# Attention's v loads: from four loads of 32 partitions to one load of 128 partitions per row group and column block

## The reference

```python
    qg = q.reshape(B, rows, GRID_W, H, dh)
    kg = k.reshape(B, rows, GRID_W, H, dh)
    vg = v.reshape(B, rows, GRID_W, H, dh)
...
        s = jnp.einsum('bqhd,brqchd->bhqrc', q_r, k_win).astype(jnp.float32) * scale + bias[None]
        p = jax.nn.softmax(s.reshape(B, H, GRID_W, wr * WIN_COLS), axis=-1)
        p = p.reshape(B, H, GRID_W, wr, WIN_COLS).astype(v.dtype)
        return jnp.einsum('bhqrc,brqchd->bqhd', p, v_win)
```

## Time and profile before

| | us |
|---|---|
| median of 3 runs (3213.3 to 3214.53) | 3214.18 |
| the profiled execution's own time | 3212.91 |
| its span in the trace | 3211.1 |
| TensorE busy in the span | 3116.0 (97%) |
| VectorE busy | 2296.2 (72%) |
| ScalarE busy | 1908.3 (59%) |

### The profile page before, as it was taken

One profiled execution on the slowest core, in us unless ns is written; L12 is line 12 of the kernel. 1 busy time (PEld: TensorE's weight loads), 2 busy tenths in 40 slices (PEclk: granted clock), 3 DMA queues, 4 the chain that ended last, 5 costly groups with the idle time before them and its releaser, 6 DMA issues.

```text
span 3211.1 us, 48845 instructions
## 1 busy us (share of the span) xinstructions
PE 3116.0 (97%) x18750; PEld 2790.3 (87%) x18750; DVE 2296.2 (72%) x3531; ACT 1908.3 (59%) x3107; POOL 187.7 (6%) x191
## 2 busy tenths in 40 slices
PE   5999999995999999999999999999999999999998
PEld 4777765785999999999999999999999999999997
DVE  4679927547777777777777777777777776777775
ACT  5154457543666666666665666666666666666654
POOL 0000000001010101010101010110101010101000
PEclk8999999997999999999999999999999999999999
DMA  9321166335666757575857576666657575857562
GB/s 333 133 66 56 50 199 237 137 119 204 240 249 239 255 211 265 200 274 193 295 201 284 211 261 230 249 248 243 247 219 257 200 277 197 295 192 287 213 248 97
DMA packets 140266, 691.17 MB, mean 215 GB/s; under 512 B 11264, under 2 KB 46352, under 8 KB 116752
## 3 DMA queue, kind: packets, MB, share of 16 engines
q1 hardware_dynamic: 130368, 661.98, 55.4%
q0 software_dynamic: 8128, 25.17, 3.2%
q10 hardware_dynamic: 1552, 1.00, 0.1%
HBM read 650.35 MB, written 37.77 MB: 214 GB/s over the span
## 4 chain that ended last, share of the span: by engine, by line
PE 75%; DVE 1%; DMA 0%; issue 0%; POOL 0%; POOLq 0%; DVEq 0%
PE psG L1671 34%; PE psG L1673 16%; PE psY L1690 5%; PE psY L1693 5%; PE psY L1691 5%; PE psY L1692 5%; PE psY L1694 5%; DMA xg<-xhat_d,isel 0%; DVE idxu L1165 0%; DVE affT L1168 0%; DVE vals L1162 0%; DVE xst L1990 0%; PE psG L1647 0%; POOL out L1736 0%; DVE yp L1938 0%
## 5 line engine op out<-in xcount | busy, mean ns | idle before, releaser
L1671 PE MATMUL psG<-xe,w_gu_hi_part 128*128 128x384 f32 x5632 | 1619.9, 358 | 2.7 <-DVE xe L2000 2.7
L1673 PE MATMUL psG<-xe,w_gu_lo_part 128*128 128x192 f32 x5632 | 1411.6, 251 | 0.0
L1673 PEld LDWEIGHTS psG<-xe,w_gu_lo_part 128*128 128x128 f32 x5632 | 1076.4, 191 | 13.1
L1671 PEld LDWEIGHTS psG<-xe,w_gu_hi_part 128*128 128x128 f32 x5632 | 1058.9, 188 | 16.5 <-DVE xe L2000 3.1
L1913 DVE TENSOR_TENSOR w_gu_lo_part<-raw_gu,w_gu_hi_part 128x1024 fp32r<-128x1024 f32 x704 | 859.3, 1223 | 119.2 <-ACT w_gu_hi_part L1795 119.2
L1795 ACT ACTIVATE w_gu_hi_part<-raw_gu 128x1024 fp32r<-128x1024 f32 x704 | 738.5, 1052 | 12.9 <-DMA raw_gu<-in_w_gu 12.9
L1823 ACT ACTIVATE low<-psG 128x384 f32<-128x384 f32 x352 | 173.0, 491 | 695.2 <-PE psG L1673 694.9
L1948 DVE TENSOR_TENSOR gu<-psG,low 128x384 f32<-128x384 f32 x352 | 196.0, 557 | 495.9 <-ACT low L1823 490.9
L1918 DVE TENSOR_TENSOR w_dn_lo_part<-raw_dn,w_dn_hi_part 128x1024 fp32r<-128x1024 f32 x352 | 431.2, 1225 | 1.0 <-ACT w_dn_hi_part L1806 0.8
L1806 ACT ACTIVATE w_dn_hi_part<-raw_dn 128x1024 fp32r<-128x1024 f32 x352 | 368.1, 1046 | 3.6 <-PE psY L1694 3.6
L1690 PE MATMUL psY<-w_dn_hi_part,hs 128*128 128x512 f32 x704 | 282.6, 401 | 0.0
(11 more groups left out here) (215 smaller groups left out, 3005.3 us busy)
## 6 DMA issues: line engine op xcount, KB each, us to landing
raw_gu<-in_w_gu SPq DMA_DIRECT2D x176, 2048.0 KB, 8.3
raw_dn<-in_w_down SPq DMA_DIRECT2D x176, 1024.0 KB, 8.6
shared<-in_ada_w SPq DMA_DIRECT2D x12, 2048.0 KB, 11.0
w_raw<-in_w_in SPq DMA_DIRECT2D x20, 512.0 KB, 5.3
bias<-in_bias SPq DMA_DIRECT2D x6, 1536.0 KB, 12.9
qk_d<-shared SPq DMA_DIRECT2D x8, 768.0 KB, 3.5
qk<-qk_d SPq DMA_DIRECT2D x8, 768.0 KB, 6.3
out<-x SPq DMA_DIRECT2D x12, 512.0 KB, 2.6
```

Source lines behind the costliest of these rows:

```text
L1671: pe.matmul(bank[:, 0:2 * CAP], wh, xe[:, k, :, :].rearrange("p a b -> p (a b)"), start=(k == 0), stop=False, skip_group_check=True)
L1673: mm = pe.matmul(bank[:, 0:CAP], wl, xe[:, k, 0, :], start=False, stop=(k == KD - 1), skip_group_check=True)
```

## The change

`load_v` now issues one DMA for one row group `n` and one column block `j`, over all 128 partitions, where before it issued four (one for each `r`) of 32 partitions that covered several row groups. The rows of the sample get two waits: row groups 2 to 4 at pair 4, row group 5 at pair 8. Both column blocks 0 and 1 are loaded at the end of `front`. The second half's loads are held until `pv` of pair 8 is done (`o_done` at 9), since they add to the same semaphore as row group 5; before, they were held until `s_done` was 24.

```diff
-                        load_v(sp, v, v_d, 0, 0, 2, 0, v_first)
+                        for j in range(2):
+                            for row in range(2):
+                                load_v(sp, v, v_d, j, row, 0, v_first)
...
-def load_v(sp, v, v_d, j, n0, n1, half, loaded):
-
-    v_rows = v_d.rearrange("(n r c) d -> r c n d", r=4, c=GRID_W)
+def load_v(sp, v, v_d, j, n, half, loaded):
+
     cols = slice(half * (WA // 2), (half + 1) * (WA // 2))
-    for r in range(4):
-        sp.dma_start(v[r * K_COLS:(r + 1) * K_COLS, :, :].rearrange("p (n j) d -> p n j d", j=COL_BLOCKS)[:, n0:n1, j, cols],
-                     v_rows[r, KEY_COL0[j]:KEY_COL0[j] + K_COLS, n0:n1, cols]).then_inc(loaded, 16)
+    sp.dma_start(v[:, n * COL_BLOCKS + j, cols],
+                 v_d.rearrange("(n r c) d -> n r c d", r=4, c=GRID_W)[n, :, KEY_COL0[j]:KEY_COL0[j] + K_COLS, cols]).then_inc(loaded, 16)
...
-                for j in range(1, COL_BLOCKS):
-                    load_v(sp, v, v_d, j, 0, 2, 0, v_loaded[j // 2])
+                for j in range(2, COL_BLOCKS):
+                    for n in range(2):
+                        load_v(sp, v, v_d, j, n, 0, v_loaded[1])
                 for j in range(COL_BLOCKS):
-                    load_v(sp, v, v_d, j, 2, 6, 0, v_loaded[2])
+                    for n in range(2, 5):
+                        load_v(sp, v, v_d, j, n, 0, v_loaded[2])
+                for j in range(COL_BLOCKS):
+                    load_v(sp, v, v_d, j, 5, 0, v_loaded[3])
...
-                sp.wait_ge(s_done, 2 * NB)
+                sp.wait_ge(o_done, 2 * COL_BLOCKS + 1)
                 for j in range(COL_BLOCKS):
-                    load_v(sp, v, v_d, j, 0, 6, 1, v_loaded[3])
+                    for n in range(6):
+                        load_v(sp, v, v_d, j, n, 1, v_loaded[3])
...
                     if u < COL_BLOCKS:
-                        pe.wait_ge(v_loaded[j // 2], 16 * 4 * 2)
+                        pe.wait_ge(v_loaded[j // 2], 16 * 4)
                     elif u == COL_BLOCKS:
-                        pe.wait_ge(v_loaded[2], 16 * 4 * COL_BLOCKS)
+                        pe.wait_ge(v_loaded[2], 16 * 3 * COL_BLOCKS)
+                    elif u == 2 * COL_BLOCKS:
+                        pe.wait_ge(v_loaded[3], 16 * COL_BLOCKS)
                     elif u == 2 * NB:
-                        pe.wait_ge(v_loaded[3], 16 * 4 * COL_BLOCKS)
+                        pe.wait_ge(v_loaded[3], 16 * 7 * COL_BLOCKS)
```

## The result

The changed kernel takes 3248.3 us, the median of 4 runs (3247.03 to 3248.79), against 3213.74 for the kernel before (4 runs, 3211.79 to 3214.53). The ratio is 1.0108, with a 95% interval of 1.0096 to 1.012: 34.6 us slower, where 3250 was predicted.

What follows compares the result with a forecast made beforehand. TensorE, busy 97%, bounds the kernel; the v stall offers at most 5.8 us. 48 loads, one store and two groups, against 520.0, cost 35.5 us: 3212.9 + 35.5 = 3248.4, median 1.3 above: 3250; range 3232 to 3285.

Steps and rivals of the forecast that it cites:

- Four engines, as the smaller side says: New v loads: 4 grid rows outermost in DRAM against 128 partitions, so 4 of 16 DMA engines carry each load.
- The same ones, in order: SP's queue: every v load uses the same four engines, which take packets in issue order, so everything issued later waits.
- The chain of landings: SP's queue in attention: loads summed in order from 455.15 to 553.7, the four engines never running dry.
- 1.54 us a load: One v load on four engines: 32 packets of 1 KB each at 48 ns; bounds 1.31 to 2.27 us.
- 11.0 us a group: q, k and two bias tiles for the next heads: 4.72 MB at 428 GB/s, 11.0 us on the queue.
- Pair 4, 13.5 us late: Pair 4's product with v waits for twelve loads of row groups 2 to 4: 488.7 against 475.19 before.
- Pair 12, 2.0 more: Pair 12's bias lands at 505.8, wanted at 503.8: 2.0 us more delay, 15.5 in all.
- Pair 24, 18.2 and 1.8 for the clock: Pair 24's q, k and bias land at 553.7, wanted at 535.5: 18.2 us more, plus 1.8 for the low clock.
- What costs nothing: Twenty issues (11 to 21 us) hidden behind 30.7 us of engine work; holding the second half and pair 8's wait free.
- Sixteen engines: Rival: sixteen engines carry each v load, gaining 0 to 5.8 us, 3208 to 3214; chance 0.13 (sixteen or eight).
- Crowded packets (71 ns): Rival: four engines with 71 ns a packet, 3285; within the 0.80 for four engines at 38 to 71 ns.
- faster ones (38): Rival: four engines at 38 ns a packet, 1.22 us a load, 3234; within the 0.80 for 38 to 71 ns.

Runs made afterwards that it cites:

- outer2: Changed kernel with each v load split in two loads of two grid rows (2 outermost on the DRAM side): 3312.54 us, ratio 1.031.
- v_behind: Changed kernel with q, k and bias for heads 4 and 5 issued ahead of the second half of v: 3240.26 us, ratio 1.0083.
- wait_per_block: Kernel before, own loads and order, with the waits for row groups 2 to 5 apart for each column block: 3213.0 us, ratio 0.9999.
- bias_early: wait_per_block with the bias of head 2 issued ahead of column blocks 2 and 3: 3209.91 us, ratio 0.9991.
- outer32: Changed kernel with 32 key columns outermost on the v loads' DRAM side, not 4 grid rows; output partly from misplaced keys: 3208.48 us, ratio 0.9982.
- old_loads_new_waits: Kernel before, its 32-partition loads kept, row group 5 loaded and waited for apart, second half held until pair 8's product: 3219.51 us, ratio 1.0023.

## Why the prediction was right

The forecast was right in its mechanism, and in its sum too, 3250 for 3248.3; that the sum came within 2 us is in part luck, as several of its terms were off and made up for each other. Point by point:

- **Four engines, as the smaller side says.** Right: 4 small packets a load, 27% share, and with 8 and 32 outermost entries the loss is gone.
- **The same ones, in order.** Right: `outer2` pays for its halves one after the other, and `v_behind` moves the stall.
- **The chain of landings.** TensorE and VectorE resume at a landing, so their rows date it:

| resumed | predicted | measured |
|---|---|---|
| product of pair 2 | 470.2 | 470.40 |
| product of pair 4 | 488.7 | 488.08 |
| bias of pair 12 | 505.8 | 506.71 |
| bias of pair 24 | 553.7 | 553.40 |

- **1.54 us a load.** Too large: 1.40 in the steady stretch, as a packet took 46 ns and not 48. That 48 came so close is luck. The earlier trace rows give 0.93 MB for 1122 packets, 829 bytes each, so they are not all packets of 1 KB: those of v's loads (692, 57 ns on average in the trace) are mixed with packets of 512 B (430, 30 ns), in which the store of v went. The nearest row for an engine alone with 1 KB packets was the earlier trace rows, 57 ns at most (48 to 49 in the trace).
- **11.0 us a group.** Too small. Between pair 12's bias and pair 24's lie 46.7 us for 24 loads and one group of q, k and bias; 24 x 1.40 = 33.6 leaves 13.1 for the group. Between pair 4 and pair 12's bias it is 18.6 - 4 x 1.40 = 13.0. The windows show that the four engines go on alone after the other twelve are done:

```profile
499.00:501.00 2.00, 1.90 (x19) 1.11 (x19) 1.52 (x7) 1.42 (x4) 0.00 (x0) 1.00 1.06 444
501.00:503.00 2.00, 1.73 (x18) 1.17 (x19) 1.00 (x4) 1.54 (x5) 0.00 (x0) 1.00 0.48 197
503.00:505.00 2.00, 1.90 (x20) 1.16 (x15) 0.00 (x0) 0.00 (x0) 0.00 (x0) 1.00 0.25 102
505.00:507.00 2.00, 0.00 (x0) 0.00 (x0) 0.29 (x1) 0.00 (x0) 0.00 (x0) 1.00 0.26 89
```

 What they carry stands in the packets from 502 to 504 us and from 504 to 506 us: up to 504 the bias (20 of 24 packets have 8 KB or more), behind that almost only the next v loads (112 of 121 packets have 1 KB).

```profile
DMA packets 24, 0.25 MB, mean 123 GB/s; under 512 B 4, under 2 KB 4, under 8 KB 4
...
DMA packets 121, 0.16 MB, mean 82 GB/s; under 512 B 5, under 2 KB 117, under 8 KB 117
```

 The rate of these windows is thus not the reason for the 2 us: a bias packet of 12 KB took 462 ns from 502 to 504 and 465 with all sixteen at work from 495 to 501 (26 GB/s an engine), and 16 packets of q and k (238 ns) with 16 of the bias make 11.2 us an engine. In the trace's packets, what is slower is v: from 489 on, with q and k on the other twelve, a packet of 1 KB took up to 72 ns (490 to 493) and not 46, some 1.3 us more on each of the four for what was left of row group 5. The rest of the 2 us is open.
- **Pair 4, 13.5 us late.** It went on at 488.08, 12.9 late, and pair 8 was 12.3 late. 20 loads at 1.40 end at 485.9, not at 488.7. 0.7 come on top because SP issued its first v load 0.7 later than in the earlier trace rows (453.31 against 452.62), which the change need not have caused: `wait_per_block` and `bias_early` have the `front` of before, and it was 1.4 and 1.2 later there. Their last packet ended at 486.5, and TensorE went on 1.6 later. The prediction took a load as landed with its last packet and had no such term.
- **Pair 12, 2.0 more.** Too small: 18.6 - 12.3 = 6.3. VectorE wanted the bias at 502.03 (506.71 - 4.68), not at 503.8, and it landed 0.9 after 505.8: 4.7 us of waiting, not 2.0 (it wanted the bias earlier because pair 8 was 12.3 late and not 13.5). Then came the low clock, which the prediction left out here and counted only at pair 24: 1.55 us for the product at 509.02 against 0.88 at 500.00, and 1.23 for the scores at 511.97 against 0.70 at 515.50.
- **Pair 24, 18.2 and 1.8 for the clock.** Too large: 34.6 - 18.6 = 16.0. What had been lost at pair 12 didn't have to be lost here, since the landing at 553.4 sets the end of both.
- **What costs nothing.** The wait at pair 8 cost nothing: no row has one. Nor do the issues show a cost of their own, as SP's 1.47 us each went at the queue's pace of 1.40, though the earlier trace rows were no rows for them: both sides of a `bias_s` load (L486) go over 128 partitions outermost, and only their inner shapes differ. But the claim that the split of the waits is free holds only for these loads; with the old ones the split made the kernel 7.4 us slower, by the 16 further issues ahead of the bias.
- **The rivals.** Sixteen engines were to give 3208 to 3214; `outer32`, which makes that case real, took 3208.48. Crowded packets (71 ns) and faster ones (38) were both off: 46.

Why did the whole stand closer than its terms? In windows of 1 us from 455 to 553 the DMA share never falls under 0.22 of the sixteen, 3.5 engines. The four are thus never idle, and only the sum of their work counts, and no stall ahead of the last adds to it. From the 553.7 of the forecast, 1.40 for 1.54 takes 6.7 us in 48 loads, two groups of 13.0 for 11.0 give 4.1 back, the later first load 0.7, and the time from the last packet to the engine that waits for it 1.6: 553.4, as measured. The groups are themselves differences of such times, so this sum says how the terms share the time and is no proof of them. Against the 520.0 at which VectorE wanted the bias before, that is 33.4 us; the other 1.2 of the 34.6 come behind the landing, where 1.8 had been put down for the clock.

## What to carry to other kernels

Look at the outermost size of both sides of a DMA, not only at the partitions: on SP's queue the small packets of a load (those under 512 B) count its engines (on GpSimd's they don't, there were 1657 in 21 us), and here 128 partitions against 4 rows made 95 GB/s out of a queue that gives over 400. On one queue such a load also slows what is issued behind it, so price the queue as a whole and look for the last consumer that waits. When a wait is shortened while the queue behind it stays full, name the next transfer in line before counting a gain: two edits here removed or shortened the wait on v (`wait_per_block`, `old_loads_new_waits`), and the bias behind it took all or more of it.

## What the runs showed of the hardware

- SP issued no faster than the engines emptied its queue: 0.54 us an issue with 16 engines behind it, 1.47 with four (1.40 us of work a load), and 56.01 us for 40 issues with two (1.40, for 1.37 us of work).
- A v load of 128 partitions against 32 DRAM rows took longer to issue than one of 32 against 32, with the engines not full (share 0.60 to 0.79 between 460 and 472 us): 0.71 us in `outer32` (14.13 / 20) against 0.54 before. Whether the unequal outermost sizes make it or the form over 128 partitions was not tried apart.
- An engine moved about 24 GB/s in 1 KB packets (48 for two, 95 for four).
- A 1 KB packet took 46 ns where four engines wrote over 128 partitions, 51 where 16 did (`outer32`, 466 to 471 us: 70.1% of 80 us for 1090 packets), and 71 where 16 wrote into 32. The crowded partitions need not be the reason for the 71: in the changed kernel v's packets over 128 partitions rose to 72, too, while the other twelve engines carried q and k.
